# One 512-column matmul per upper weight tile, and loops written out, in a fp32r-split transformer block on one core

## The chip, the core and the metric

The kernel runs on one core of a Trainium2 chip. The metric is device time in microseconds (us), lower is better; the kernel before took 3140.52 us (median of three runs, 3138.92 to 3140.62).

## The reference, cut to what matters

Two transformer-like blocks on 256 tokens with 2048 features, batch 1. The first block is a mixer (a gated delta rule with 8 heads beside a 31-tap convolution), a cross attention over 256 memory tokens and a squared-ReLU MLP:

```python
h = h + hybrid_mixer(rms_norm(h, g), w_in, ...)           # 2048 -> 6160 columns, and w_out
h = h + memory_cross_attention(rms_norm(h, g), mem_n, ...) # four 2048 x 2048 weights
h = h + squared_relu_mlp(rms_norm(h, g), w1, w2)           # 2048 -> 8192 -> 2048
```

The second takes 256 context tokens as well, scales and shifts its norms by a modulation vector (`c @ w_mod`), has latent attention, neighbourhood attention and a Fourier part, an output projection, and a gated MLP with 3-tap convolutions (2048 -> 2 x 5632 -> 2048). All is float32, and nearly all of the work is activations (256 tokens) times weights that are each used once.

## The kernel before, in words

Weights stream from HBM in slots of 128 x 1024 float32 (`raw`, 8 buffers, 906 slots). A float32 product is made of three products in the type fp32r. ScalarE copies a slot to fp32r (`whi`, line 836), VectorE subtracts that from `raw` to get the lower part (`wlo`, line 1233), 4 buffers each. The activations lie in `act` (for the second matrix of each MLP in `hid`) as two parts [P, 2, 16, 256]. For each 128 x 128 weight tile TensorE adds up `whi` x upper, `whi` x lower and `wlo` x upper, three matmuls of 256 columns at line 458, into 256 columns of a bank. In phases marked `flip` the activations are the stationary side and the weight slots are streamed.

A `Phase` is one matrix: `nblocks` blocks of 256 output features, each two halves `hf` of 128, over `chunks` of 128 input features; four chunks are a slot, so a block of a 2048-row matrix takes four slots, 32 tiles and 96 matmuls. Two blocks alternate between banks 0 and 1. A body has `per_body` blocks; a phase of more than one body runs in a hardware loop (`Fori`) on each engine, one of a single body is straight-line code.

`over` writes ScalarE's and VectorE's side of a phase: slot after slot, with the first three slots of a phase split before the phase before is evicted, and a block's eviction `LAG` = 3 slots behind its last slot. Each engine works in this order, so a split written behind an eviction waits for it. Evictions:
- `to`: ScalarE copies the bank to SBUF and frees it (`block_free`).
- `conv4` (phase `qkv`): ScalarE scales the bank by the last tap into `ev` (line 869), VectorE adds three more taps from the bank for each half (line 1252, six instructions) and frees it, ScalarE applies SiLU (line 873).
- `glu`: ScalarE takes the sigmoid of one half (line 880), VectorE multiplies (line 1266).
- `resid`: VectorE adds the bank to `h` (line 1283, or 1287 with a gate); ScalarE squares the result in the last phase ahead of a norm.
- `relu2` (phases `w1`): ReLU, square, upper part on ScalarE, lower part on VectorE.
- `gated` (phases `up`): ScalarE scales and adds a bias (line 901), VectorE adds two taps for each half (line 1308), SiLU (line 906), then product and split on VectorE.

Beside the phases `glu`, `qkv`, `z_0` and `z_1` VectorE also computes the 31-tap convolution (`conv31`, line 1438), one chunk of 128 channels per body, whose first step copies the input (line 1426). Beside `memk` to `w2_3` it sums the modulation (`mod_chunk`, line 1219), with a short group of matmuls (line 476) once in each body.

In order the phases are `glu` (8 blocks), `qkv` (12), `z_0`, `z_1` (2 each), the delta rule, `wout`, `memk`, `memv`, `wq`, cross attention, `wo`, four rounds of `w1` and `w2` (8 blocks each), the small ones of the second block (`ckv`, `nak`, `nav`, `kr` for context and tokens, `cq`, `naq`, `fn`), local attention, `kn` and `v` twice, `qn`, `qr`, latent attention, `wout2`, and three rounds of `up` (16, 16, 12 blocks) and `down` (8 blocks over 16, 16, 12 chunks).

Of the kernel before, what the change touches and what calls it, by code (L numbers as in the profile page):

```python
# [11 lines left out]
ds = bass.ds  # L12


P = 128
# [112 lines left out]
def build(nc, x_t, mem_t, ctx_t, stream, mods, pvec, eye, cmix, catt, na_bias, na_mask, out_t):  # L128
    es = ExitStack()
    with es:  # L130
# [8 lines left out]
        whi = sb("whi", [P, SPL_N, SLOT], F32R)  # L139
        wlo = sb("wlo", [P, SPL_N, SLOT], F32R)  # L140
# [58 lines left out]
        bank = [es.enter_context(nc.psum_tensor(f"bank{i}", [P, 512], F32)) for i in range(8)]  # L199
# [24 lines left out]
        ev_v = sem("ev_v")  # L224
        act_step = sem("act_step")
# [54 lines left out]
        class Chain:  # L280


            def __init__(self, eng, s):
                self.eng, self.s, self.n, self.i, self.per = eng, s, 0, 0, 0

            def __call__(self, ins):
                ins.then_inc(self.s, 1)
                self.n += 1
                self.eng.wait_ge(self.s, self.i * self.per + self.n)
# [6 lines left out]
            def now(self):  # L296
                return self.i * self.per + self.n

            def loop(self, i, per):

                self.n, self.i, self.per, self.mark = self.n - per, i, per, self.n

            def end(self, iters):

                assert self.n == self.mark, (self.n, self.mark)
                self.n, self.i, self.per = self.n + self.per * (iters - 1), 0, 0
# [4 lines left out]
        def over(eng, ph, slot_of, evac_fn, chain, links, extra=None):  # L311
# [21 lines left out]
            if ph.iters > 1:  # L333
                with eng.Fori(1, ph.iters) as i:
                    chain.loop(i, links)
                    body(i, False, 0)
                chain.end(ph.iters)
# [9 lines left out]
        def _(sp):  # L347
# [10 lines left out]
            def bodies(first, last, mod=False):  # L358
                with sp.Fori(first, last) as b:
# [69 lines left out]
        def _(pe):  # L429
            c = Counts(pe)  # L430

            def phase(ph, src, c0=0, after=None):
# [3 lines left out]
                def body(i):  # L436
                    for k in range(ph.K):
                        b = bank[(ph.block0 + k) % 2]

                        pe.wait_ge(block_free, i * ph.K + (ph.block0 + k + 1))  # L440
                        for sl in range(ph.slots_per_block):
# [6 lines left out]
                            for ci in range(ph.per_slot):  # L448
                                kc = sl * ph.per_slot + ci
                                for hf in range(ph.ncol // P if not ph.flip else TT):  # L450
                                    for n, (wx, ax) in enumerate(((whi, 0), (whi, 1), (wlo, 0))):
                                        if ph.flip:
                                            lhs = src[:, ax, c0 + kc, hf * P:(hf + 1) * P]
                                            rhs = wx[:, buf, ci * NCOL:(ci + 1) * NCOL]
                                        else:
                                            lhs = wx[:, buf, ci * ph.ncol + hf * P:ci * ph.ncol + (hf + 1) * P]
                                            rhs = src[:, ax, c0 + kc, :]
                                        mm = pe.matmul(b[:, hf * T:(hf + 1) * T], lhs, rhs,  # L458
                                                       start=(kc == 0 and hf == 0 and n == 0),
                                                       stop=(kc == ph.chunks - 1 and n == 2), skip_group_check=True)  # L460
# [3 lines left out]
                if ph.iters > 1:  # L464
# [324 lines left out]
            for n in range(3):  # L789
                for mt in range(TT):  # L790
                    mm = over_features(bank[5 + n][:, mt * P:(mt + 1) * P], ROOT, 2 * n + mt, mt == 0)
# [34 lines left out]
        def _(sc):  # L826
# [16 lines left out]
            def to(dst, flip=False, func=ACT.Copy):  # L843
                def make(ph):
                    def f(n, b, k):
                        done(ph, n)
                        o = dst[:, 0:TT, ds(n * NCOL, NCOL)] if flip else dst[:, ds(n * 2, 2), :]
                        sc.activation(o, b2(b), func).then_inc(block_free, 1)
# [3 lines left out]
            def one(dst):  # L852
                def make(ph):
                    def f(n, b, k):
                        done(ph, n)
                        sc.activation(dst, bank[b][:, 0:T], ACT.Copy).then_inc(block_free, 1)
# [5 lines left out]

            def conv4(ph):
# [12 lines left out]
            def glu(ph):  # L876
                def f(n, b, k):
                    done(ph, n)
                    sc.wait_ge(block_free, n + (FREE + ph.block0))
                    sc.activation(ev[:, 0, 0:T], b2(b)[:, 1, :], ACT.Sigmoid).then_inc(ev_a, 1)  # L880
                return f

            def relu2(ph):
                def f(n, b, k):
                    done(ph, n)
                    c.at(ev_v, n + EV0)
                    sc.activation(ev[:, 0, :], bank[b][:, :], ACT.Relu).then_inc(block_free, 1)
                    sc.wait_ge(block_free, n + (FREE + ph.block0 + 1))
                    chain(sc.activation(ev[:, 1, :], ev[:, 0, :], ACT.Square))
                    sc.activation(hid[:, 0, ds(n * 2, 2), :], ev[:, 1, :].rearrange("p (a b) -> p a b", a=2),  # L890
                                  ACT.Copy).then_inc(ev_a, 1)
# [995 lines left out]
```

## Time and profile before

| | |
|---|---|
| median of the runs | 3140.52 us |
| profiled execution, span from first to last instruction | 3137.8 us |
| mean granted TensorE clock | 0.972 |
| TensorE matmuls busy | 2967.8 us, 95% |
| VectorE busy | 2097.9 us, 67% |
| ScalarE busy | 1331.5 us, 42% |
| HBM read | 585.88 MB |

TensorE's matmuls are pipelined, so its busy share says that there was always a matmul in flight, not that it ran at its peak; the time from one start to the next has to be worked out from stretches and counts. The chain that ended last tells which work followed on which. Idle time of the other engines costs nothing as long as TensorE finds its slots split and its banks free.

### The profile page before, as it was taken

Reading aid. Unit: us, or ns where it says so; the run is one execution under the profiler, and the core shown is the slowest. Engines: PE = TensorE matmul, PEld = TensorE weight load, DVE = VectorE, ACT = ScalarE, POOL = GpSimd, SP = SyncE. Lnnn points to the kernel's source line nnn. Section 1 sums busy time; section 2 is a strip of 40 time slices with the busy share of each in tenths; the row PEclk is TensorE's granted clock in tenths of the full one; section 3 lists DMA queues with packets and bytes.
Section 4 is the critical chain, followed back from the end, with each engine's and each line's share of the span. In section 5 each row is a group of like instructions: output and inputs, shape, how many; then the busy total and the mean of one; then the engine's idle time right before and its main releaser. Section 6 shows DMA issues by size and latency. Waiting matters only on the chain.

```text
span 3137.8 us, 61329 instructions
## 1 busy us (share of the span) xinstructions
PE 2967.8 (95%) x23858; PEld 2904.4 (93%) x23858; DVE 2097.9 (67%) x2934; ACT 1331.5 (42%) x1646; POOL 5.1 (0%) x13
## 2 busy tenths in 40 slices
PE   7999888999999899999999989979998999999998
PEld 7998788999998899999999979959498999999998
DVE  6988654698877777676776775445456665665565
ACT  4445323343433443444435444435344443444443
POOL 0000000000000000000000000000000000000000
PEclk9999898999999999999999989998899999999999
DMA  5554102577655677777777745514054555556553
GB/s 198 177 171 162 54 1 92 186 265 255 243 201 184 245 277 274 278 275 264 281 268 264 278 132 168 183 60 135 20 181 142 180 195 184 183 187 193 182 185 117
DMA packets 160343, 589.92 MB, mean 188 GB/s; under 512 B 17840, under 2 KB 17840, under 8 KB 159696
## 3 DMA queue, kind: packets, MB, share of 16 engines
q1 hardware_dynamic: 159264, 579.93, 53.8%
q0 software_dynamic: 944, 8.12, 0.7%
q8 instruction: 94, 1.54, 0.2%
q14 instruction: 41, 0.34, 0.0%
HBM read 585.88 MB, written 2.10 MB: 187 GB/s over the span
## 4 chain that ended last, share of the span: by engine, by line
PE 87%; DVE 8%; ACT 3%; issue 2%; DMA 1%; DVEq 0%; SPq 0%; ACTq 0%
PE bank L458 77%; PE bank L725 1%; DVE wlo L1233 1%; PE bank L476 1%; PE bank L482 1%; PE bank L629 1%; DVE modacc L1438 1%; DVE tmp L1388 1%; PE bank L486 1%; DVE ev L1252 1%; PE bank L627 1%; PE bank L621 1%; PE bank L700 1%; DVE ev L1355 1%; ACT whi L836 1%
## 5 line engine op out<-in xcount | busy, mean ns | idle before, releaser
L458 PE MATMUL bank<-act,whi 128*128 128x256 f32 x10144 | 1854.2, 286 | 56.8 <-DVE wlo L1233 16.8
L458 PEld LDWEIGHTS bank<-act,whi 128*128 128x128 f32 x10144 | 1599.7, 194 | 61.8 <-issue 39.5
L1233 DVE TENSOR_TENSOR wlo<-raw,whi 128x1024 fp32r<-128x1024 f32 x906 | 1098.3, 1223 | 538.6 <-ACT whi L836 535.0
L458 PE MATMUL bank<-act,wlo 128*128 128x256 f32 x5072 | 1445.9, 285 | 0.0
L836 ACT ACTIVATE whi<-raw 128x1024 fp32r<-128x1024 f32 x906 | 947.9, 1056 | 918.2 <-PE bank L458 913.0
L458 PEld LDWEIGHTS bank<-act,wlo 128*128 128x128 f32 x5072 | 983.0, 194 | 0.0
L458 PE MATMUL bank<-hid,whi 128*128 128x256 f32 x3456 | 597.1, 278 | 0.0
L458 PEld LDWEIGHTS bank<-hid,whi 128*128 128x128 f32 x3456 | 524.6, 188 | 0.0
L458 PE MATMUL bank<-hid,wlo 128*128 128x256 f32 x1728 | 480.0, 278 | 0.0
L1219 DVE SCALAR_TENSOR_TENSOR modacc<-modraw,small,modacc 128x512 f32<-128x512 f32 x480 | 348.5, 747 | 12.3 <-DMA modraw<-mods 6.9
L458 PEld LDWEIGHTS bank<-hid,wlo 128*128 128x128 f32 x1728 | 324.7, 188 | 0.0
L458 PE MATMUL bank<-whi,act 128*128 128x256 f32 x896 | 161.9, 283 | 0.0
L458 PEld LDWEIGHTS bank<-whi,act 128*128 128x128 f32 x896 | 139.5, 192 | 0.0
L1308 DVE SCALAR_TENSOR_TENSOR ev<-bank,pv,ev 128x255 f32<-128x255 f32 x176 | 76.9, 479 | 92.8 <-ACT ev L901 86.9
L458 PE MATMUL bank<-wlo,act 128*128 128x256 f32 x448 | 126.8, 283 | 0.0
L1438 DVE SCALAR_TENSOR_TENSOR modacc<-modraw,modacc 128x256 f32<-128x256 f32 x232 | 98.6, 480 | 0.3
L458 PEld LDWEIGHTS bank<-wlo,act 128*128 128x128 f32 x448 | 85.8, 192 | 0.0
L901 ACT ACTIVATE ev<-bank,pv 128x256 f32<-128x256 f32 x88 | 44.9, 561 | 91.0 <-PE bank L458 91.0
L914 ACT ACTIVATE ev<-h 128x512 f32<-128x512 f32 (+1 forms) x40 | 25.3, 632 | 117.3 <-DVE h L1283 68.0
L1297 DVE TENSOR_TENSOR hid<-ev,hid 128x512 fp32r<-128x512 f32 x32 | 22.2, 693 | 75.2 <-ACT hid L890 75.2
L906 ACT ACTIVATE ev<-ev 128x256 f32<-128x256 f32 x44 | 18.4, 418 | 89.3 <-DVE ev L1308 89.3
L621 PE MATMUL bank<-tmp 128*128 128x128 f32 x224 | 33.3, 298 | 15.5 <-DVE tmp L1541 8.6
(269 smaller groups left out, 1524.1 us busy)
## 6 DMA issues: line engine op xcount, KB each, us to landing
raw<-stream SPq DMA_DIRECT2D x906, 512.0 KB, 4.5
modraw<-mods SPq DMA_DIRECT2D x192, 512.0 KB, 4.6
h<-x_t SPq DMA_DIRECT2D x4, 512.0 KB, 6.0
memV<-mem_t POOLq DMA_DIRECT2D x1, 2048.0 KB, 9.7
tmp<-ctx_t POOLq DMA_DIRECT2D x1, 2048.0 KB, 12.2
out_t<-tmp SPq DMA_DIRECT2D x4, 512.0 KB, 2.6
cz<-catt POOLq DMA_DIRECT2D x1, 1216.0 KB, 13.2
bias<-na_bias POOLq DMA_DIRECT2D x1, 1024.0 KB, 5.7
```

The costliest lines, as they stand in the source:

```text
L458: mm = pe.matmul(b[:, hf * T:(hf + 1) * T], lhs, rhs, start=(kc == 0 and hf == 0 and n == 0), stop=(kc == ph.chunks - 1 and n == 2), skip_ ...
L476: mm = pe.matmul(bank[2][:, 4 * w + n:4 * w + n + 1], modacc[:, w, n * P:(n + 1) * P], ones[:, 0:1], start=True, stop=True, skip_group_che ...
L482: return pe.matmul(out, src[:, tok], ones[:, 0:1], start=start, stop=stop, skip_group_check=True)
L486: return pe.matmul(out, small[:, col + n:col + n + 1].to_broadcast([P, P]), ident[:, :], start=start, stop=True, skip_group_check=True)
L621: mm = pe.matmul(bk(hg, 0)[:, n, :], MT[hg][:, n, :], X[hg][:, n, :], start=True, stop=True)
L627: pe.matmul(bk(hg, 2)[:, n, :], XT[hg][:, n, :], Y[hg][:, n, :], start=True, stop=True)
L836: sc.activation(whi[:, at % SPL_N, :], raw[:, at % RAW_N, :], ACT.Copy).then_inc(hi_done, 1)
L901: ins = sc.activation(ev[:, 0, hf * T:(hf + 1) * T], b2(b)[:, hf, :], ACT.Identity, scale=par("ff_conv", n * 6 + (6 * first + 3 * hf + 1)) ...
L1219: ins = ve.scalar_tensor_tensor(acc, wt, col, acc, ALU.mult, ALU.add)
L1233: ve.tensor_tensor(wlo[:, at % SPL_N, :], raw[:, at % RAW_N, :], whi[:, at % SPL_N, :].bitcast(F32), ALU.subtract).then_inc(split_done, 1)
L1308: ins = ve.scalar_tensor_tensor(o, b2(b)[:, hf, so], par("ff_conv", n * 6 + (6 * first + 3 * hf + j)), o, ALU.mult, ALU.add)
L1438: ins = ve.scalar_tensor_tensor(acc, x_, w, acc, ALU.mult, ALU.add)
```

## The change

`whi` and `wlo` become halves of one tensor `w2`. For each weight tile the upper part is multiplied by both activation parts at once: one matmul of 512 columns whose moving side is `act[:, :, kc, :]`, into a whole bank; the left half gets upper x upper, the right half upper x lower. The second matmul adds lower x upper (256 columns) to the right half. In `flip` phases the roles are exchanged: 512 columns of `w2[:, :, buf, cols]` are streamed over the upper activations, then 256 of `whi` over the lower. A block needs a bank for each half `hf`, so two blocks take four banks, 0 and 1 and 6 and 7 (`STREAM`), and each eviction has to add the two halves of its banks (`main` and `rest`).

The evictions change so: ScalarE copies `main` and VectorE adds `rest` and frees the banks (`to` with `add`, `one`). In `conv4`, `glu`, `relu2` and `gated` this copy and add come first, in `ev`, and what follows reads SBUF: the scaling by the last tap, the sigmoid, the bias now wait for VectorE's add. `relu2` does ReLU and square in one VectorE instruction. `resid` becomes two passes in a row on `h`. The SiLU of `zT` moves from its evictions to two instructions on ScalarE ahead of the delta rule. All loops (`Fori`) are written out on all engines. Two banks for spreading roots change (5, 2, 4 for 5, 6, 7).

```diff
-                                    for n, (wx, ax) in enumerate(((whi, 0), (whi, 1), (wlo, 0))):
-                                        if ph.flip:
-                                            lhs = src[:, ax, c0 + kc, hf * P:(hf + 1) * P]
-                                            rhs = wx[:, buf, ci * NCOL:(ci + 1) * NCOL]
-                                        else:
-                                            lhs = wx[:, buf, ci * ph.ncol + hf * P:ci * ph.ncol + (hf + 1) * P]
-                                            rhs = src[:, ax, c0 + kc, :]
-                                        mm = pe.matmul(b[:, hf * T:(hf + 1) * T], lhs, rhs,
...
+                                    out = bank[b + hf]
+                                    if ph.flip:
...
+                                        pe.matmul(out[:, :], src[:, 0, c0 + kc, tok], w2[:, :, buf, cols],
+                                                  start=kc == 0, stop=False, skip_group_check=True)
+                                        mm = pe.matmul(out[:, T:2 * T], src[:, 1, c0 + kc, tok], w2[:, 0, buf, cols],
+                                                       start=False, stop=kc == ph.chunks - 1, skip_group_check=True)
+                                    else:
+                                        at = ci * ph.ncol + hf * P
+                                        pe.matmul(out[:, :], w2[:, 0, buf, at:at + P], src[:, :, c0 + kc, :],
+                                                  start=kc == 0, stop=False, skip_group_check=True)
+                                        mm = pe.matmul(out[:, T:2 * T], w2[:, 1, buf, at:at + P], src[:, 0, c0 + kc, :],
+                                                       start=False, stop=kc == ph.chunks - 1, skip_group_check=True)
...
-                if ph.iters > 1:
-                    with pe.Fori(0, ph.iters) as i:
-                        body(i)
-                else:
-                    body(0)
+                for i in range(ph.iters):
+                    body(i)
```

ScalarE's side of `conv4`, and VectorE's side of it and of `to`:

```diff
                     done(ph, n)
-                    sc.wait_ge(block_free, n + (FREE + ph.block0))
+                    sc.activation(halves(ev[:, 1, :]), main(b), ACT.Copy).then_inc(ev_a, 1)
+                    sc.wait_ge(block_free, n + (FREE + ph.block0 + 1))
                     for hf in range(2):
-                        ins = sc.activation(ev[:, 0, hf * T:(hf + 1) * T], b2(b)[:, hf, :], ACT.Copy,
+                        ins = sc.activation(ev[:, 0, hf * T:(hf + 1) * T], ev[:, 1, hf * T:(hf + 1) * T], ACT.Copy,
                                             scale=par("dn_conv", n * 8 + (4 * hf + 3)))
                     ins.then_inc(ev_a, 1)
-                    sc.wait_ge(block_free, n + (FREE + ph.block0 + 1))
-                    chain(sc.activation(qkvT[:, ds(n * 2, 2), :], ev[:, 0, :].rearrange("p (a b) -> p a b", a=2), ACT.Silu))
+                    c.at(taps_done, n + 1)
+                    chain(sc.activation(qkvT[:, ds(n * 2, 2), :], halves(ev[:, 0, :]), ACT.Silu))
...
+            def add(dst, flip=False):
+
+                def make(ph):
+                    def f(n, b, k):
+                        c.at(ev_a, n + 1)
+                        o = dst[:, 0:TT, ds(n * NCOL, NCOL)] if flip else dst[:, ds(n * 2, 2), :]
+                        ve.tensor_tensor(o, rest(b), o, ALU.add).then_inc(block_free, 1)
...
             def conv4(ph):
                 def f(n, b, k):
-                    c.at(ev_a, n + 1)
+                    c.at(ev_a, n * 2 + 1)
+                    ve.tensor_tensor(halves(ev[:, 1, :]), rest(b), halves(ev[:, 1, :]), ALU.add).then_inc(block_free, 1)
+                    c.at(ev_a, n * 2 + 2)
```

ScalarE's side of `glu`, `relu2` and `gated`, and VectorE's `resid` and `relu2`:

```diff
+                    sc.activation(halves(ev[:, 1, :]), main(b), ACT.Copy).then_inc(ev_a, 1)
+                    sc.wait_ge(block_free, n + (FREE + ph.block0 + 1))
+                    sc.activation(ev[:, 0, 0:T], ev[:, 1, T:2 * T], ACT.Sigmoid).then_inc(ev_a, 1)
...
-                    sc.activation(ev[:, 0, :], bank[b][:, :], ACT.Relu).then_inc(block_free, 1)
-                    sc.wait_ge(block_free, n + (FREE + ph.block0 + 1))
-                    chain(sc.activation(ev[:, 1, :], ev[:, 0, :], ACT.Square))
+                    sc.activation(halves(ev[:, 0, :]), main(b), ACT.Copy).then_inc(ev_a, 1)
+                    c.at(taps_done, n + 1)
...
+                        sc.activation(halves(ev[:, 1, :]), main(b), ACT.Copy).then_inc(ev_a, 1)
+                        sc.wait_ge(block_free, n + (FREE + ph.block0 + 1))
...
-                            ve.tensor_tensor(h[:, ds(n * 2, 2), :], b2(b), h[:, ds(n * 2, 2), :], ALU.add).then_inc(block_free, 1)
+                            o = h[:, ds(n * 2, 2), :]
+                            chain(ve.tensor_tensor(o, main(b), o, ALU.add))
+                            ve.tensor_tensor(o, rest(b), o, ALU.add).then_inc(block_free, 1)
...
+                    ve.tensor_tensor(halves(ev[:, 0, :]), rest(b), halves(ev[:, 0, :]), ALU.add).then_inc(block_free, 1)
+                    ve.wait_ge(block_free, n + (FREE + ph.block0 + 1))
+                    ve.scalar_tensor_tensor(ev[:, 1, :], ev[:, 0, :], 0.0, ev[:, 0, :], ALU.max, ALU.mult).then_inc(taps_done, 1)
...
+            sc.wait_ge(block_free, FREE + PH["z_1"].block0 + PH["z_1"].nblocks)
+            for n in range(2):
+                sc.activation(zT[:, 4 * n:4 * n + 4, :], zT[:, 4 * n:4 * n + 4, :], ACT.Silu)
```

## Rows read from the trace of the kernel before

**Rows 1.** The page: busy times, chain by line, an instruction queue, the stream's DMAs.

```profile
PE 2967.8 (95%) x23858; PEld 2904.4 (93%) x23858; DVE 2097.9 (67%) x2934; ACT 1331.5 (42%) x1646; POOL 5.1 (0%) x13
...
PE bank L458 77%; PE bank L725 1%; DVE wlo L1233 1%; PE bank L476 1%; PE bank L482 1%; PE bank L629 1%; DVE modacc L1438 1%; DVE tmp L1388 1%; PE bank L486 1%; DVE ev L1252 1%; PE bank L627 1%; PE bank L621 1%; PE bank L700 1%; DVE ev L1355
...
q8 instruction: 94, 1.54, 0.2%
...
raw<-stream SPq DMA_DIRECT2D x906, 512.0 KB, 4.5
```

**Rows 2.** Chain in order of time: start, length (us), matmul count; one-body phases, `up`, `down`, `w2`.

```profile
1944.90 110.16 PE bank L458 x918
...
2649.94 180.12 PE bank L458 x1501
...
2560.97 85.11 PE bank L458 x751
...
1165.96 29.13 PE bank L458 x257
...
1211.90 31.80 PE bank L458 x270
```

**Rows 3.** Groups of line 458 that read `wlo`: count | busy us, mean ns.

```profile
L458 PE MATMUL bank<-act,wlo 128*128 128x256 f32 x5072 | 1445.9, 285 | 0.0
L458 PE MATMUL bank<-hid,wlo 128*128 128x256 f32 x1728 | 480.0, 278 | 0.0
L458 PE MATMUL bank<-wlo,act 128*128 128x256 f32 x448 | 126.8, 283 | 0.0
```

**Rows 4.** Chain in order of time: float32 matmuls of 256 columns, then of one.

```profile
336.53 3.45 PE bank L567 x16
...
339.99 3.48 PE bank L482 x31
```

**Rows 5.** TensorE's timeline at the start of `glu`; then busy times and clock, `w1_0`.

```profile
40.23 0.41 PE L458 MATMUL bank<-act,wlo 128*128 128x256 f32 x1
...
40.87 0.41 PE L458 MATMUL bank<-act,wlo 128*128 128x256 f32 x1
...
1066.00:1151.00 85.00, 84.90 (x692) 84.93 (x693) 61.90 (x74) 43.28 (x50) 0.53 (x1) 0.97 0.76 280
```

**Rows 6.** Timelines of ScalarE and of VectorE in `qkv`: start, length (us), instructions.

```profile
197.66 0.63 ACT L873 ACTIVATE qkvT<-ev 128x512 f32 x1 [5.35 <-DVE ev L1252]
198.41 3.90 ACT L836 ACTIVATE whi<-raw 128x1024 fp32r<-128x1024 f32 x4
204.07 0.84 ACT L869 ACTIVATE ev<-bank,pv 128x256 f32<-128x256 f32 x2 [1.76 <-PE bank L458]
...
199.50 1.23 DVE L1233 TENSOR_TENSOR wlo<-raw,whi 128x1024 fp32r<-128x1024 f32 x1 [1.98 <-ACT whi L836]
...
207.21 2.68 DVE L1252 SCALAR_TENSOR_TENSOR ev<-bank,modraw,ev 128x255 f32<-128x255 f32 x6
```

**Rows 7.** VectorE's timeline in `glu`: the first step of two bodies' convolution.

```profile
57.00 0.30 DVE L1426 COPY modraw<-cin 128x286 f32 x1
...
104.93 0.30 DVE L1426 COPY modraw<-cin 128x286 f32 x1
```

**Rows 8.** Groups of instructions: an add and a copy of 512 columns from a bank.

```profile
L1283 DVE TENSOR_TENSOR h<-bank,h 128x512 f32<-128x512 f32 (+1 forms) x48 | 33.2, 691 | 18.4 <-PE bank L458 18.2
L848 ACT ACTIVATE kN<-bank 128x512 f32<-128x512 f32 x8 | 4.8, 599 | 13.0 <-PE bank L458 13.0
```

**Rows 9.** Timelines in `up_0`: ScalarE's first pass of an eviction, VectorE's next splits.

```profile
2480.20 1.02 ACT L901 ACTIVATE ev<-bank,pv 128x256 f32<-128x256 f32 x2 [2.12 <-PE bank L458]
...
2485.10 3.49 DVE L1233 TENSOR_TENSOR wlo<-raw,whi 128x1024 fp32r<-128x1024 f32 x3
```

**Rows 10.** Stretches: length; busy PE, PEld, DVE, ACT, POOL; clock, DMA share, GB/s.

```profile
661.00:709.00 48.00, 48.00 (x404) 48.00 (x403) 39.91 (x49) 19.06 (x21) 0.00 (x0) 1.00 0.81 283
...
1153.00:1197.00 44.00, 44.00 (x386) 44.00 (x386) 33.01 (x38) 18.44 (x19) 0.00 (x0) 1.00 0.81 286
```

More of the change, by code:

```diff
@@ L296, in now, with over @@
             def now(self):
[L297 to L306, printed above, removed]
+                return self.n
         block = es.enter_context(nc.Block())
-        def over(eng, ph, slot_of, evac_fn, chain, links, extra=None):
+        def over(ph, slot_of, evac_fn, extra=None):
             ends = [(k + 1) * ph.slots_per_block - 1 + LAG for k in range(ph.K)]
@@ L332, in over @@
             body(0, True, min(PRE, ph.S) if n else 0)
-            if ph.iters > 1:
[L334 to L337, printed above, removed]
+            for i in range(1, ph.iters):
+                body(i, False, 0)
             after = order[n + 1] if n + 1 < len(order) else None
@@ L358, in bodies @@
             def bodies(first, last, mod=False):
-                with sp.Fori(first, last) as b:
+                for b in range(first, last):
                     for j in range(RAW_N):
@@ L951, in _ @@
             phase("glu", glu)
-            phase("qkv", conv4, PH["qkv"].K)
+            phase("qkv", conv4)
+            c.end(taps_done, PH["qkv"].nblocks)
             def row(r):
@@ L1111, in _ @@
             for r in range(FF1_ROUNDS):
-                phase(f"w1_{r}", relu2, PH["w1_0"].K)
+                phase(f"w1_{r}", relu2)
                 c.end(ev_v, PH["w1_0"].nblocks)
+                c.end(taps_done, PH["w1_0"].nblocks)
                 phase(f"w2_{r}", squared if r == FF1_ROUNDS - 1 else nothing)
@@ L1134, in _ @@
             phase("fn", to(fT))
-            phase("kr_x", one(kr[:, 0, :]))
+            phase("kr_x", one(kr[:, 0:1, :]))
             attention("na", 8)
@@ L1259, in f @@
                         if j < DN_TAPS - 1:
-                            ve.wait_ge(dve_step, chain.i * chain.per + chain.n)
+                            ve.wait_ge(dve_step, chain.now())
                 return f
@@ L1323, in gated, with phase @@
                 return make
[L1325 removed]
+            def phase(name, evac, extra=None):
                 ph = PH[name]
[L1327 removed]
+                over(ph, slot, evac(ph), extra)
             def residual(name, gate=None, extra=None):
@@ L1444, in conv31 @@
                 return f
-            CONV_LINKS = 1 + CF_TAPS + 1
             before_qkv = PH["glu"].iters - 1
-            phase("glu", glu, CONV_LINKS, conv31(PH["glu"], -1))
-            c.end(ev_a, 8)
-            phase("qkv", conv4, PH["qkv"].K * 5 + 1 + CONV_LINKS, conv31(PH["qkv"], before_qkv, stage=True))
-            c.end(ev_a, 12)
+            phase("glu", glu, conv31(PH["glu"], -1))
+            c.end(ev_a, 16)
+            phase("qkv", conv4, conv31(PH["qkv"], before_qkv, stage=True))
+            c.end(ev_a, 24)
             for mt in range(TT):
@@ L1454, in _ @@
             ins.then_inc(gate_dve, 1)
-            phase("z_0", nothing, 0, conv31(PH["z_0"], before_qkv + PH["qkv"].iters))
+            phase("z_0", add(zT[:, 0:4, :]), conv31(PH["z_0"], before_qkv + PH["qkv"].iters))
+            c.end(ev_a, PH["z_0"].nblocks)
             c.at(gate_act, 1)
@@ L1461, in _ @@
             ins.then_inc(gate_dve, 1)
-            phase("z_1", nothing, 0, conv31(PH["z_1"], before_qkv + PH["qkv"].iters + 1))
+            phase("z_1", add(zT[:, 4:8, :]), conv31(PH["z_1"], before_qkv + PH["qkv"].iters + 1))
+            c.end(ev_a, PH["z_1"].nblocks)
             assert before_qkv + PH["qkv"].iters + 2 == 8
@@ L1586, in _ @@
             norm(memory, g("norm_mem"))
-            phase("memk", nothing, 0, h_norm(4))
-            phase("memv", nothing)
+            phase("memk", add(memK), h_norm(4))
+            c.end(ev_a, PH["memk"].nblocks)
+            phase("memv", add(memV, flip=True))
+            c.end(ev_a, PH["memv"].nblocks)
             norm(h, g("norm_xa"), ahead=True)
-            phase("wq", nothing)
+            phase("wq", add(tmp))
+            c.end(ev_a, PH["wq"].nblocks)
             def attention(kind, c0=0):
@@ L1635, in _ @@
                 phase(f"w1_{r}", relu2)
-                c.end(ev_a, PH["w1_0"].nblocks)
+                c.end(ev_a, 2 * PH["w1_0"].nblocks)
                 if r == FF1_ROUNDS - 1:
@@ L1737, in _ @@
             for r, n in enumerate(FF2_ROUNDS):
-                phase(f"up_{r}", gated(first), 2 * 5)
-                c.end(ev_a, 2 * n)
+                phase(f"up_{r}", gated(first))
+                c.end(ev_a, 3 * n)
                 first += n
```

164 lines of the change are left out of this document (99 added, 65 removed).

## Prediction

> **What bounds the kernel now.** First the page's busy line and its chain that ended last: TensorE is busy 95% of the span and the streamed matmuls of line 458 alone make 77% of the chain [rows 1]. Busy time says little for a pipelined engine, so next the chain in order of time, divided by its counts: 1501 matmuls in 180.12 us are 120.0 ns each, 918 in 110.16 us again 120.0 ns; where the moving tile is `hid`, 113.3 ns (751 in 85.11 us, 257 in 29.13 us) or 117.8 ns (270 in 31.80 us) [rows 2]. These stretches have no gap. At the full clock of 2.4 GHz, 256 columns take 106.7 ns, so a stretch runs 6.6 to 13.3 ns above its columns for every matmul. Elsewhere another engine sets the pace: in `qkv` the matmuls wait on VectorE and ScalarE (below).
>
> **Part 1, the matmuls.** A 128x128 weight tile costs three matmuls of 256 columns with three weight loads, 3 x 120 = 360 ns on `act`. After the change it is one of 512 and one of 256: the same 768 columns (320 ns), one instruction and one load less. So the columns save nothing, only what stands above them. The trace has no 512-column fp32r matmul. The nearest rows: a float32 matmul pass that occupies the array 213.3 ns, with a weight load each, repeats every 3.45/16 = 215.6 ns; one-column matmuls, which only their loads bound, repeat every 3.48/31 = 112.3 ns [rows 4]. So a load (112) hides wholly under 213 ns, but not quite under 107. I price the 512-column matmul at 215.7 and the 256-column one at today's 120, because the load of the next upper tile can only start beside it: 336 ns a tile, 24 ns less. On `hid` the short one keeps its 113.3 (`down`) or 113.3 to 117.8 ns (`w2`, about 116.1 as a mean: the first 12 of its 32 slots run at the lower rate), so 329 against 340 and 332 against 348.
> The Trainium skill (TensorE: Matmul & The Clock Gate, Back-to-back issue gap) gives columns/2.4 + 2.5 ns, 109.2 and 215.8 ns: an estimate by it is 327.6 ns a tile before and 325.0 after, 2.6 ns saved, which speaks against this change. The trace disagrees for the short matmul (120.0) and agrees for the long one (215.6).
> Counts: the `wlo` rows give one per tile, 5072 + 448 = 5520 tiles on `act` and 1728 on `hid` [rows 3]. Of the first, `glu`, `qkv` and `z` have 24 blocks x 32 = 768, where TensorE will not be the bound; 4752 are left. At the granted half clock (1.2 GHz) a tile takes 0.64 us [rows 5], purely its 768 columns, and that stays. `w1_0` ran at a mean clock of 0.97 over 85 us [rows 5], some 5 us or 8 tiles at half clock; seven such starts make about 60 tiles. Saving: 4692 x 24 = 112.6 us; `w2` 4 x 256 x 16.6 = 17.0; `down` 704 x 11 = 7.7. Sum 137 us.
> Bounds of the tile on `act`: 329 (the short one at the 113.3 seen on `hid`), and 347, if 13.3 ns belong to each load that runs beside a full-rate stream (320 + 2 x 13.3). I take 336, nearest to the two rows.
>
> **Part 2, the mixer's projections.** In `qkv` each block goes round a ring: SiLU on ScalarE (197.66), first split (198.41), VectorE's four lower splits with convolution taps between (199.50 to 207.21), six taps of `conv4` (2.68), SiLU again: 12.4 us [rows 6], against 4 x 8 x 360 ns = 11.5 us of matmuls. TensorE is already late here. The change puts into this ring a VectorE add of 512 columns (0.69, the row of line 1283 [rows 8]) and behind it the two scalings that ran beside VectorE before and now need the sum (0.84 us [rows 6], about 0.95 with both hand-overs). ScalarE's copy of the main halves lies ahead, beside the splits. Round: about 14.0 us, +1.6 x 12 = +19 us. TensorE then needs 10.75 of 14.0 us, so nothing of part 1 shows here.
> In `glu` VectorE's bodies take (104.93 - 57.00)/2 = 24.0 us [rows 7] against 23.0 of matmuls. Twice an add and a wait for the sigmoid behind it (0.42, as a pass of 256 columns in [rows 6], and hand-overs; it was ready before) give 26.2 us a body: +6 over three, less 1 where the first body, without taps, runs faster. `z_0` and `z_1`, one such body each: matmuls 21.5, VectorE as in `glu`, with adds but without the sigmoid, +1. Part 2: +25 us. Bounds: +13, if the bubbles close and only the adds count; +35, if each round also loses a further hand-over.
>
> **Part 3, evictions elsewhere.** Every block gets a ScalarE copy (0.60) and an add (0.69) where it had one [rows 8]; residual blocks get a second pass. Four slots of splits stand ahead of TensorE, so throughput and the time to the next split decide. Throughput: the densest stretch, with the modulation sums, has VectorE busy 39.9 of 48.0 us [rows 10]; with 4 x 0.69 more it is 42.7 of 16 x 8 x 336 ns + 1.68 = 44.7 us. Close, still cover. DMA moves 286 GB/s in `w2` at 0.81 share [rows 10]; 4% faster is 0.85. Time: the gated eviction has the longest chain. Before, from ScalarE's first pass at 2480.20 to VectorE's next split at 2485.10, 4.9 us [rows 9]. Queued behind it on both engines is the split that TensorE wants 3 x 2.69 = 8.06 us after the block's end. The change adds copy 0.65 and add 0.75: 6.3, split finished at 7.5. It just hides, 0.5 us to spare; without that cover it is 44 blocks x the excess. In `relu2` 1.3 us are added to 3.2: hidden. Cost 0.
> Not hidden, since nothing else is ready: the last block of `wout`, `wo`, `w2_3`, `wout2`, `down_2` (five second passes) and of `wq`, `kr_x`, `qr` ahead of attention (three adds), 0.75 each = 6.0; at the end of `z_1` copy and add, 1.4; the SiLU of `zT`, two passes of 1024 columns moved ahead of the delta rule and partly beside VectorE, 1.2. Sum 8.6 us.
>
> **Part 4, loops written out.** TensorE's loops cost nothing now: the 1501 matmuls at 120.0 ns run over their turns. Straight-line code, the phases of one body, runs at the same 120.0 (918 matmuls) [rows 2], so its fetching is hidden there, at half the DMA load of `w2`. Priced 0. New banks (0,1 and 6,7): 0, the waits between phases stand.
>
> **Sum.** -137 + 25 + 9 = -103 us. The profiled execution's span was 3137.8 us, 2.7 below the median of 3140.5; so 3034.5 in a profile and 3037 as median.
>
> **Rivals.**
> A. The excess belongs to loads beside a full-rate stream (347 a tile). For it: `act` and `hid` differ at equal shape, which looks like two reads disturbing each other; the excess is gone at half clock. Against: the fp32 pass with a load each shows 2.3 ns. Time: 4692 x 13.3 = 62, `hid` about 14, so -76 + 34 = 3098. The same page (What happens when you issue a matmul) says the load has a read port of its own and takes none from the stream, which speaks against A; no row here isolates it.
> B. The short matmul also recovers, since the load is never late behind a long one: 329 on `act`: -145 - 28 + 34, 3001 us; with part 2 at its low end 2989.
> C. Slower: the excess grows with columns streamed (a moving read that stalls every few elements). Then 768 columns still cost 360 ns, part 1 is nil, and parts 2 and 3 stay: 3174. It decides as soon as the tile stays above 355 ns. Against it: the short fp32 passes; but they read at half the rate.
> D. Slower: straight-line code at 0.8 DMA share starves an engine. The larger instruction queue moved 94 packets [rows 1]; written out I estimate twice as many. If 28 of them leave TensorE waiting for one landing, 4.5 us in the row of the stream's DMAs [rows 1], that is +125: 3162. Against it: nothing at 0.53 share.
> E. By the skill's gap rule, as a mechanism: the short matmul's 120 would have to be chance; 7248 x 2.6 = 19 saved, 3155. The rows at 120.0 contradict it.
> F. The eviction chains turn out longer and `up` and `w1` stall 1 us a block: 76 blocks, 3037 + 76 = 3113.
>
> **How the numbers follow.** Forecast 0.50 (its own 3015 to 3060), A 0.18, B 0.12, F 0.05, C 0.07, D 0.05, E 0.03. A measurement tells 0.2%, 6.3 us, from no change. Faster: 0.85; slower: C, D, E, 0.14, with 0.01 left for the same. Range 2985 to 3113: it takes in B's low end, A with part 2 at its high end and F, and leaves 0.15 to 0.2 outside.
>
> **What the profile will show.** Right: in `up` two matmuls a tile at 216 and 120 ns, 16 blocks in about 172 us; rounds of 14 us in `qkv` with TensorE waiting on line 1233's successor; 3 us less for a body of `w1`; no gap in `up`. Wrong: a start-to-start of 240 or more for the long matmul (C), 227 (A); VectorE waits inside `up` (F); "issue" ahead of weight loads (D).

## The result, and the profile after

| | before | after |
|---|---|---|
| median of 8 runs each, us | 3140.57 (3138.28 to 3142.02) | 3148.13 (3144.65 to 3153.37) |
| ratio, 95% interval | | 1.0022 (1.0014 to 1.0031) |
| span of the profiled execution, us | 3137.8 | 3146.3 |

The change makes the kernel 0.2% slower; 3037 us was forecast, and 3148 lies above the range. The page of the changed kernel, its lines that answer to [rows 1] and [rows 3] (busy times with counts; chain by line; the queue that moves instructions; groups of instructions):

```profile
PE 2939.3 (93%) x16610; PEld 2538.8 (81%) x16610; DVE 2283.2 (73%) x3244; ACT 1340.6 (43%) x1679; POOL 5.1 (0%) x13
...
PE psum L458 44%; PE psum L460 22%; DVE w L1242 4%; PE psum L452 3%; DVE modacc L1481 2%; PE psum L454 2%; DVE modacc L1228 1%; PE psum L723 1%; DVE ev L1281 1%; ACT w L834 1%; PE psum L627 1%; PE psum L480 1%; DVE tmp L1431 1%; PE psum L474 1%; PE psum L625 1%
...
L458 PE MATMUL psum<-act,w 128*128 128x512 f32 x5072 | 1816.0, 402 | 81.7 <-DVE w L1242 40.8
L460 PE MATMUL psum<-act,w 128*128 128x256 f32 x5072 | 1434.0, 283 | 0.0
...
q8 instruction: 131, 2.15, 0.3%
```

A third of the streamed matmuls and their loads are gone (23858 to 16610 with all others), yet TensorE is busy for only 28 us less. Its share of the chain falls from 87% to 80%, and VectorE's splits rise in it from 1% to 4%. Line 458 idles 81.7 us, of which a split of VectorE ends 40.8, most of it in `qkv`. The start-to-start times say the rest. TensorE's timeline in `down_2` (start, length in us), then the instructions of line 458 in `up_1` and in `cq`:

```profile
3073.05 0.40 PE L458 MATMUL psum<-hid,w 128*128 128x512 f32 x1
3073.29 0.28 PE L460 MATMUL psum<-hid,w 128*128 128x256 f32 x1
3073.41 0.40 PE L458 MATMUL psum<-hid,w 128*128 128x512 f32 x1
3073.64 0.28 PE L460 MATMUL psum<-hid,w 128*128 128x256 f32 x1
3073.76 0.40 PE L458 MATMUL psum<-hid,w 128*128 128x512 f32 x1
```

```profile
L458 PE MATMUL psum<-act,w x454: 395/398/403, 2664.9 to 2825.0; 128*128 128x512 f32 x152
...
L458 PE MATMUL psum<-act,w x64: 391/391/391, 1998.7 to 2020.5; 128*128 128x512 f32 x64
```

The first fence has two tiles in 0.71 us; over the phase a tile takes 353 ns, 235 from the start of the long matmul to the start of the short and 118 to the next long one. The second is a view of line 458 in a stretch (count, shortest, median and longest duration in ns, first and last start): in `up_1` 453 steps of a tile in 160.1 us, 353.4 ns each; in `cq` 63 in 21.8 us, about 347 ns (230 and 117). On `act` a tile was 360, so it lost 7 to 13 ns, not 24; on `hid` it was 340 in `down` and about 348 in `w2`, and became 353. Nothing waits in these stretches: the fault is inside the stream.

The rate can also change within a phase. In `w1_1` a short group of modulation matmuls stands between these two stretches of the same code:

```profile
L458 PE MATMUL psum<-act,w x80: 395/398/403, 1274.9 to 1302.8; 128*128 128x512 f32 x80
...
L458 PE MATMUL psum<-act,w x102: 392/394/395, 1309.7 to 1344.7; 128*128 128x512 f32 x102
```

Ahead of the group 79 steps take 27.9 us, 353 ns each; behind it 101 take 35.0 us, 347 ns.

Phase starts, read from the first matmul of each in the two traces: `qkv` 132.3 to 137.9, `wout` 514.8 to 539.7, `w1_0` 1066.1 to 1086.1, `up_0` 2374.5 to 2379.9, last matmul of `down_2` 3122.2 to 3129.5. So 25 us are lost up to `wout`, some 20 are won back until `up_0`, and `up` and `down` together give 2 us away.

### The profile page after: what moved, and what is told of

It is laid out like the page before. It is cut to its first block, busy times and chain, and to the rows that moved or that the text cites. A ratio compares the mean times of both kernels' runs of the same rounds, so it can differ in the third digit from the quotient of the medians.

```text
span 3146.3 us, 41040 instructions
## 1 busy us (share of the span) xinstructions
PE 2939.3 (93%) x16610; PEld 2538.8 (81%) x16610; DVE 2283.2 (73%) x3244; ACT 1340.6 (43%) x1679; POOL 5.1 (0%) x13
## 4 chain that ended last, share of the span: by engine, by line
PE 80%; DVE 14%; ACT 4%; issue 1%; DMA 0%; SPq 0%; DVEq 0%; ACTq 0%
PE psum L458 44%; PE psum L460 22%; DVE w L1242 4%; PE psum L452 3%; DVE modacc L1481 2%; PE psum L454 2%; DVE modacc L1228 1%; PE psum L723 1%; DVE ev L1281 1%; ACT w L834 1%; PE psum L627 1%; PE psum L480 1%; DVE tmp L1431 1%; PE psum L474 1%; PE psum L625 1%
## 5 line engine op out<-in xcount | busy, mean ns | idle before, releaser
L458 PE MATMUL psum<-act,w 128*128 128x512 f32 x5072 | 1816.0, 402 | 81.7 <-DVE w L1242 40.8
L460 PE MATMUL psum<-act,w 128*128 128x256 f32 x5072 | 1434.0, 283 | 0.0
L1242 DVE TENSOR_TENSOR w<-raw,w 128x1024 fp32r<-128x1024 f32 x906 | 1095.3, 1221 | 340.5 <-ACT w L834 338.3
L834 ACT ACTIVATE w<-raw 128x1024 fp32r<-128x1024 f32 x906 | 933.8, 1054 | 777.4 <-PE psum L460 716.2
L458 PEld LDWEIGHTS psum<-act,w 128*128 128x128 f32 x5072 | 968.4, 191 | 322.2 <-DVE w L1242 41.1
L460 PEld LDWEIGHTS psum<-act,w 128*128 128x128 f32 x5072 | 973.5, 192 | 0.0
L458 PE MATMUL psum<-hid,w 128*128 128x512 f32 x1728 | 611.9, 398 | 0.5 <-DVE hid L1364 0.5
L460 PE MATMUL psum<-hid,w 128*128 128x256 f32 x1728 | 485.6, 281 | 0.0
L458 PEld LDWEIGHTS psum<-hid,w 128*128 128x128 f32 x1728 | 324.9, 188 | 80.6 <-issue 0.8
L460 PEld LDWEIGHTS psum<-hid,w 128*128 128x128 f32 x1728 | 324.4, 188 | 0.0
L452 PE MATMUL psum<-w,act 128*128 128x512 f32 x448 | 158.1, 397 | 0.0
L452 PEld LDWEIGHTS psum<-w,act 128*128 128x128 f32 x448 | 84.1, 188 | 20.1
L454 PEld LDWEIGHTS psum<-w,act 128*128 128x128 f32 x448 | 84.7, 189 | 0.0
```

Source lines behind the costliest of these rows:

```text
L452: pe.matmul(out[:, :], src[:, 0, c0 + kc, tok], w2[:, :, buf, cols], start=kc == 0, stop=False, skip_group_check=True)
L454: mm = pe.matmul(out[:, T:2 * T], src[:, 1, c0 + kc, tok], w2[:, 0, buf, cols], start=False, stop=kc == ph.chunks - 1, skip_group_check=True)
L458: pe.matmul(out[:, :], w2[:, 0, buf, at:at + P], src[:, :, c0 + kc, :], start=kc == 0, stop=False, skip_group_check=True)
L460: mm = pe.matmul(out[:, T:2 * T], w2[:, 1, buf, at:at + P], src[:, 0, c0 + kc, :], start=False, stop=kc == ph.chunks - 1, skip_group_check ...
L834: sc.activation(whi[:, at % SPL_N, :], raw[:, at % RAW_N, :], ACT.Copy).then_inc(hi_done, 1)
L1242: ve.tensor_tensor(wlo[:, at % SPL_N, :], raw[:, at % RAW_N, :], whi[:, at % SPL_N, :].bitcast(F32), ALU.subtract).then_inc(split_done, 1)
```

## The experiments

**Loops alone.** Before with its loops written out and nothing else.

```
-                with eng.Fori(1, ph.iters) as i:
+                for i in range(1, ph.iters):
-                with sp.Fori(first, last) as b:
+                for b in range(first, last):
-                if ph.iters > 1:
-                    with pe.Fori(0, ph.iters) as i:
-                        body(i)
-                else:
-                    body(0)
+                for i in range(ph.iters):
+                    body(i)
```

> The kernel before with nothing changed but the loops written out on all engines. If straight-line code costs nothing (my pricing): 3140 us, within 3 of before. If its fetching is what ate the gain of the matmuls: 3170 us or more.

Measured 3136.91 us, ratio 0.999 (0.9981 to 1.0). Its page:

```profile
q8 instruction: 188, 3.08, 0.4%
```

Twice the packets of [rows 1], and no time lost. Rival D falls.

**The parts of a tile alone.** A kernel of matmuls only, with the rest of the computation left out: once ScalarE has filled the buffers (by 33.5 us), ScalarE, VectorE and the queues are idle. It and the three kernels of its kind below ran once each.

> This kernel leaves the whole computation out: TensorE alone runs stretches of matmuls on fixed data, each stretch a source line of its own, with a weight load before every matmul and ScalarE, VectorE and the DMAs idle. Theory 1 (the stall above 2.4 GHz goes with the columns of the moving fp32r tile, about 10%): 512 columns take 235 ns and 256 take 118 wherever they stand, one piece or two, whether or not the weight tile changes; bfloat16 takes 109 and 216. Theory 2 (the stall goes with each weight load that runs beside a full-rate stream): the excess over the columns is the same 13 to 17 ns for 512 and for 256 columns, so 512 alone takes 227 to 230 ns. Theory 3 (VectorE, ScalarE and DMA traffic in SBUF cause it): with them idle 256 columns take 109 and 512 take 216 ns.

The chain, and then the view of its one line of matmuls in five stretches (count; ns; first and last start; forms):

```profile
33.54 231.42 PE psum L67 x1532
```

```profile
L67 PE MATMUL psum<-act,w x192: 283/283/283, 42.8 to 65.7; 128*128 128x256 f32 x192
...
L67 PE MATMUL psum<-act,w x128: 277/340/403, 65.8 to 88.2; 128*128 128x256 f32 x64, 128*128 128x512 f32 x64
...
L67 PE MATMUL psum<-act,w x59: 389/389/397, 89.7 to 102.9; 128*128 128x512 f32 x59
...
L67 PE MATMUL psum<-hid,w x180: 279/279/280, 133.8 to 154.9; 128*128 128x256 f32 x180
...
L67 PE MATMUL psum<-hid,w x122: 279/338/398, 156.7 to 178.1; 128*128 128x512 f32 x61, 128*128 128x256 f32 x61
```

Three short ones on `act`: 191 steps in 22.9 us, 120 ns each, 360 a tile. Pairs on `act`: one short matmul and 63 pairs from 65.8 to 88.2 us, 353 ns a tile. The long one alone: 58 steps in 13.2 us, 227 ns. On a `hid` 36 bytes off: 117.8 ns, 353 a tile, pairs again 353. These are the kernel's figures with nothing else at work, so no other engine and no DMA makes them, and theory 3 falls. The long one alone is theory 2's; the pair is 7 ns above the 227 + 120 that theory 2 gives. The stretch with a single weight tile also takes 227.

**Undo the merge only.** After, its 512-column matmul made of two of 256; evictions, loops and banks stay as in after.

```
-  pe.matmul(out[:, :], w2[:, 0, buf, at:at + P], src[:, :, c0 + kc, :], ...)
+  for u in range(2):
+      pe.matmul(out[:, u * T:(u + 1) * T], w2[:, 0, buf, at:at + P], src[:, u, c0 + kc, :], ...)
```

> The changed kernel with its 512-column matmul made as two of 256 columns into the two halves of the bank, each with its load; all else as changed. Theory 1 (stall by columns): the tile stays at 353 to 360 ns and the time at 3148 to 3170 us. Theory 2 (stall by loads): a third load adds 13 to 17 ns to 6500 tiles, 3235 to 3260 us.

Measured 3181.97 us, 1.0133 (1.0116 to 1.0149), span 3178.3: 360 ns a tile on `act`, 340 in `down`. That is above theory 1's range and far below theory 2's: the third load costs 7 ns a tile, not 13 to 17. It takes the sum apart. Merging is worth 34 us (3182 to 3148), all the rest of the change costs 41 (3141 to 3182). Phase by phase against after: `up_1` 184.18 to 180.78 us, `wout2` 92.14 to 90.44, `w1_1` 93.81 to 91.11, but `w2_1` 90.76 to 92.09 and `down_1` 86.95 to 90.33.

**Undo the mixer's part.** After, with `glu` and `qkv` as before: three matmuls a tile, their evictions reading the banks.

```
+OLD = ('glu', 'qkv')
+  if ph.name in OLD:
+      for n, (wx, ax) in enumerate(((0, 0), (0, 1), (1, 0))):
+          mm = pe.matmul(bank[b][:, hf * T:(hf + 1) * T], w2[:, wx, buf, at:at + P], src[:, ax, c0 + kc, :], ...)
```

> The changed kernel with glu and qkv as before the change: three matmuls of 256 columns into one bank and the old evictions without the add. If my part 2 was sized right, the time falls by 23 to 27 us to about 3123 us; if the ring of qkv is not what lost the time there, it stays near 3148.

Measured 3123.53 us, 0.9953 (0.9936 to 0.9969). Part 2 costs 24.6 us, where 25 was worked out. The ring, seen in after on ScalarE and VectorE:

```profile
212.19 0.63 ACT L875 ACTIVATE qkvT<-ev 128x512 f32<-128x512 f32 x1 [2.77 <-DVE ev L1281]
218.36 0.60 ACT L868 ACTIVATE ev<-psum 128x512 f32<-128x512 f32 x1 [1.60 <-PE psum L460]
222.38 0.91 ACT L871 ACTIVATE ev<-ev,pv 128x256 f32<-128x256 f32 x2 [3.43 <-DVE ev L1276]
226.07 0.63 ACT L875 ACTIVATE qkvT<-ev 128x512 f32<-128x512 f32 x1 [2.77 <-DVE ev L1281]
...
221.66 0.69 DVE L1276 TENSOR_TENSOR ev<-psum,ev 128x512 f32<-128x512 f32 x1
223.33 2.70 DVE L1281 SCALAR_TENSOR_TENSOR ev<-ev,modraw 128x255 f32<-128x255 f32 x6 [0.98 <-ACT ev L871]
```

SiLU to SiLU is 13.88 us (212.19 to 226.07), against 12.4 in [rows 6]: the add at 221.66, and the scalings that now follow it (222.38), stand in the round.

**And the stages on `hid`.** The same, with `w2` and `down` as before too.

```
-OLD = ('glu', 'qkv')
+OLD = ('glu', 'qkv', 'w2_0', 'w2_1', 'w2_2', 'w2_3', 'down_0', 'down_1', 'down_2')
```

> The kernel e3_old_mix with w2 and down also as before the change (three matmuls, one bank, one pass onto h). In the profile after, a body pair of w2 took 92.1 us against 90.8 before and down 90.3 against 87.0. If the pair is the dearer one on hid wherever it stands: 4 x 1.3 + 2 x 3.4 + 3.3 + about 1 for the last pass = 16 us less than e3, 3107 us. If down and w2 were slower for their evictions: no change from e3's 3123.

Measured 3110.85 us, 0.9898 (0.9881 to 0.9915). The chain in `down_0`:

```profile
2542.57 87.05 PE psum L453 x768
```

768 matmuls at 113.3 ns, 340 a tile: in `down_0` and `down_1` the pair was a loss of 3.4 us each, and without it and without the longer ring the change would have been worth 1%. But the time expected here, 3107, was met in part by luck. The chain in `w2_0` and in `w2_1`, one code on the same addresses:

```profile
1157.18 35.38 PE psum L453 x312
...
1339.27 36.75 PE psum L453 x312
```

`w2_0` starts at 113.4 ns a matmul, `w2_1` at 117.8, 353 a tile; so do `w2_2`, `w2_3` and nearly all of `down_2` (68.46 us, as with pairs). There three short matmuls cost what a pair costs. The rest of the difference between the two traces comes from phases that the edit does not touch: `up_1` and `up_2` ran at 347 ns a tile instead of 353 (6 us less), `up_0` and those before it gave most of that back.

**What decides the 120.** Alone again, each shape and each shift of a buffer on a line of its own; then the same with shifts crossed with the pair and with one or two small float32 matmuls ahead; then with fewer weight columns. The rest of the computation is left out in all three.

> Again only TensorE stretches on fixed data, the whole computation left out, each stretch on lines of its own. The first such kernel gave 120.0 ns for 256 columns alone, 226.7 for 512 alone (both 13.3 above their columns), 109 and 216 for bfloat16, and 353.2 for the pair of 512 and 256, which is 6.5 more than 226.7 + 120.0. If the excess is one stall of 13.3 ns per float32 load beside a full-rate stream and a phase between the load's and the stream's reads adds the rest, the order U0 U1 L0 L1 (two long, then two short) gives 346.7 a tile or anything between 340 and 353, and moving the stream or the weights by a few elements in SBUF changes the 120.0 to other values between 107 and 120, such as the 113.3 seen on hid. If addresses play no part, all stretches of 256 columns stay at 120.0 and the order changes nothing: 353.

> TensorE stretches on fixed data, the whole computation left out: three of 256 columns per tile, and the pair of 512 and 256, with the moving tile 0 to 144 elements behind an address that is a multiple of 1 KB like the weights', each stretch twice behind one or two small float32 matmuls. In the stretches before, 256 columns alone took 120.0 ns at offsets 0 and 64, 113.3 at 4 and 16, 116 to 123 at others. If the relative address sets the stall: three at 4 or 16 take 340 ns a tile against 360 at 0, the pair 333 against 347 to 355. If the address works only for a single repeated form: no difference between offsets in three or pair.

> TensorE stretches on fixed data, the whole computation left out: fp32r streams of 256, 384 and 512 columns with loads of 32, 64, 96 and 128 weight columns, and bfloat16 beside them. If the excess of 13.3 ns is the load's own reading taken from the stream, it shrinks with the columns loaded (about 6.7 at 64, 3 at 32) and is the same at 256, 384 and 512. If it is a fixed cost of an fp32r matmul instruction, it stays 13.3 at 32 weight columns. bfloat16: 2.5 ns throughout.

First kernel: chain (start, us, line, count), then lines by first and last start:

```profile
42.31 15.36 PE psum L73 x128
57.67 14.53 PE psum L77 x64
72.20 13.99 PE psum L81 x128
86.19 13.81 PE psum L85 x64
...
172.80 7.88 PE psum L129 x64
...
188.16 7.25 PE psum L139 x64
...
210.63 7.25 PE psum L154 x64
...
256.02 7.26 PE psum L184 x64
```

```profile
L89 PE MATMUL psum<-act,w x64: 395/398/582, 99.7 to 122.1; 128*128 128x512 f32 x64
...
L218 PE MATMUL psum<-act,w x64: 392/395/579, 344.8 to 366.8; 128*128 128x512 f32 x64
```

Lines 73 and 77 are fp32r, 256 and 512 columns alone: 120.0 and 227.0 ns. Lines 81 and 85 are bfloat16: 109.3 and 215.8. So the price that I gave the long matmul is right for another type. Line 129 shifts the moving tile by 1 element: 123.1 ns. Lines 139 and 154 shift it by 4 and by 16, line 184 shifts the weights by 16: 113.3 ns each. A shift by 64 elements (256 bytes), of either, gives 120 again. Lines 89 and 218 are one piece of code, pairs on the same addresses: 22.4 us for 63 steps and later 22.0, each with a first step of about 0.54 us; past it a tile takes 353 ns and later 347. The order is no lever either: two tiles' long ones, then their short ones, 348 ns a tile; short before long 347, no better than the second stretch in the usual order (the 344.9 and 355.0 that an expectation below names are 347 and 353 in this trace).

Second kernel, the same reading: pairs at a shift of 4 behind one and behind two small matmuls, three short ones at a shift of 48 likewise.

```profile
L135 PE MATMUL psum<-acts,w x40: 387/387/482, 113.4 to 127.0; 128*128 128x512 f32 x40
...
L144 PE MATMUL psum<-acts,w x24: 398/398/482, 127.7 to 136.1; 128*128 128x512 f32 x24
...
L305 PE MATMUL psum<-acts,w x40: 276/276/365, 322.2 to 335.6; 128*128 128x256 f32 x40
...
L315 PE MATMUL psum<-acts,w x24: 281/281/364, 336.3 to 344.5; 128*128 128x256 f32 x24
```

The first tile of each takes some 0.44 us. Past it, pairs take 347 ns and 360 at one shift, three short ones 340 and 353. What ran just before a stream sets its rate for the 24 to 40 tiles of these stretches: pairs differed so at six of eleven shifts, three short ones at three. Over the eleven shifts three short ones took 340 to 360 ns and pairs 347 to 360: of 22 stretches of pairs five at 347, sixteen at 349 to 353, one at 360. The 333 that was expected for a pair at a shift of 4 or 16 did not come.

Third kernel: 256 columns with 32, 64, 96, 128 weight columns, then 384 columns with 128, 512 with 32 and with 128:

```profile
43.77 7.54 PE psum L73 x64
51.31 7.26 PE psum L77 x64
58.57 7.42 PE psum L81 x64
65.99 7.67 PE psum L85 x64
...
107.06 11.11 PE psum L101 x64
...
118.17 14.83 PE psum L105 x64
...
162.44 14.52 PE psum L117 x64
```

117.8, 113.4, 115.9 and 119.8 ns: a quarter of the weights to load is hardly cheaper, and at 512 columns 32 weight columns (line 105, 231.7 ns) are dearer than 128 (226.9), so the excess is not the length of the load. With 128 weight columns 173.6 ns for 384 and 226.9 for 512: about 13.3 ns above the columns at each length. In an even stream the excess goes by the matmul, not by its columns. Every matmul of these streams has a load of its own, so a fixed price of a load and one of a matmul are not told apart.

**Move the buffer in the kernel.** If 120 is a matter of addresses, before has it too, and needs no pairs. `act` moved by 16 elements, what follows it kept in place by a second pad.

```
+        sb("pad_a", [P, 16])
         act = sb("act", [P, 2, DC, T], F32R)
+        sb("pad_b", [P, 240])
```

> The kernel before with act moved by 16 elements (64 bytes) in SBUF and everything behind it kept at its place modulo 1 KB by a second pad; nothing else. If the relative address of stream and weights sets the stall: 5520 tiles on act x 20 ns = 110 us, less where TensorE is not the bound (768 tiles) and at half clock, so 94 us: 3046 us. If addresses play no part in the real kernel: 3140.

Measured 3107.36 us, 0.9881 (0.9858 to 0.9904), 33 us for the 94 expected; its four runs spread over 17 us (3096.79 to 3113.72), and the traced one is the slowest of them. Its chain in `w1_2` and from `up_0` to the end of `down_2`:

```profile
1466.06 45.34 PE bank L460 x384
...
2348.56 747.93 PE bank L460 x6336
```

118.1 ns a matmul where before has 120.3 (46.18 us), not 113.3: on these addresses the stream settles at 353 ns a tile in most phases and at 340 in some. The long chain has the length of before's (747.95 in its trace), though `up_1` fell from 184.18 to 180.79 us: `down_1` rose from 86.95 to 90.33, with `hid` and its weights where they were but for 1 KB. The 26 us that this execution gained stand at the start of `up_0` already (2374.5 to 2348.6): they come from the phases ahead of `up`.

**The same pads in after, and a smaller one in before** (4 and 252 elements), **and the order of the pair** (short before long in after).

> The changed kernel with the same two pads. If the address sets the stall, the pair on act falls from about 353 to about 333 ns: 4690 x 20 = 94 us, 3054 us. If addresses play no part: 3148.

> The kernel before with act moved by 4 elements (16 bytes) instead of 16. In the stretches alone, three per tile took 350 or 340 ns there, by what ran before them, against 353 at 16 and 360 at 0. If the real kernel follows: 3075 to 3105 us, below e5's 3107. If only multiples of 64 bytes help: about 3140.

> The changed kernel with the 256-column matmul of each tile ahead of the 512-column one. In the stretches alone this order took 344.9 ns a tile against 348.4 and 355.0 for the changed kernel's, but the value hangs on what ran before. If the order holds the lower value: -6 ns x 6400 tiles, 3110 us. If only the state at a stretch's start decides: 3140 to 3155, values between 347 and 357 spread as before.

Pads in after: 3161.73 us, 1.0066 (1.0049 to 1.0083), where 3054 was expected if the address decided; pairs take 353 ns nearly everywhere, also in `cq` (349 in `wout2`). Small pad in before: 3116.62, 0.992 (0.9903 to 0.9937), above the 3105 expected; 350 to 355 ns on `act`, but 355 in `down`. Short first: 3149.31, 1.0029 (1.0018 to 1.0041), tiles at 347 and 353 ns: the order brings nothing. No placement and no order brought the pair in the kernel below 347 ns.

## Why the prediction was wrong

**Part 1, the price of the long matmul: the step that failed.** "I price the 512-column matmul at 215.7", from a float32 pass [rows 4]. It measured 226.7 alone and 230 to 236 in pairs. The two rows said 215.6 for 256 columns at the half rate and 120.0 for 256 at the full one; the excess of the type at hand was 13.3, and I gave the long matmul 2.3 because it was long. The figure for the short one (120) was about right (117). Terms, from the phases of the split kernel against after: `act` -46 us where -113 stood, `w2` +5 for -17, `down` +9 for -8; together -32 for -137, the difference of the two spans. The sign on `hid` is the instructive part: its 113.3 was a favourable case of the old stream, which the old stream also lost without a change of its own (the moved `act` lost it in `down`; with the stages on `hid` undone, three short matmuls lost it from `w2_1` on), and the pair did not inherit it.

The Trainium skill (TensorE: Matmul & The Clock Gate, Back-to-back issue gap) gives columns/2.4 + 2.5 ns. The bfloat16 streams agree (109.3, 215.8); the fp32r ones do not (120.0, 226.7). The 215.6 that the prediction took as agreeing was a float32 pass of 256 columns, no 512-column matmul of the type at hand. So rival E fell as a mechanism, though its 3155 us was the nearest to the measured time: it had the saving at 19 us for 32 measured.

**The rivals.** A (347 ns a tile) describes `cq`, `naq`, `fn` and the 13.3 ns per matmul of even streams. Of its reason, the load beside the stream, the part that could be tested does not hold: fewer weights to load leave the excess. Its 3098 missed three things: `hid` dearer by 14 us instead of cheaper by 14 (28), 353 instead of 347 in `up` and elsewhere (16), part 3 (7); with them 3149. C had the right question and the wrong size: it "decides as soon as the tile stays above 355", the kernel has 353, and the split kernel with its 360 ran 3182 where C said 3174. The chance of slower, 0.14, was too low: the bounds of the tile, 329 to 347, left out that the excess in a mixed stream can be larger than in an even one (33.3 ns a tile for 26.7).

**Part 2** held: 24.6 us for 25, a round of 13.88 us for 14.0. By phase starts of the split kernel against before, `glu` cost 4.3 us where 5 stood and `qkv` 17.2 for 19.

**Part 3** held where it was argued closely and was too small in sum. The gated eviction in `up`, answering to [rows 9]:

```profile
2484.59 0.60 ACT L903 ACTIVATE ev<-psum 128x512 f32<-128x512 f32 x1 [1.71 <-PE psum L460]
...
2490.49 3.49 DVE L1242 TENSOR_TENSOR w<-raw,w 128x1024 fp32r<-128x1024 f32 x3
```

5.9 us from copy to next split (6.3 forecast), and no gap on TensorE: in the split kernel, with the new evictions, `up_1` takes the 184.18 us of before. F falls. But what was not hidden cost 41 - 25 = 16 us, not 9. The split kernel's lag on before, read from phase starts, is 24.8 us at `wout`, grows by 9.2 us until `w1_0` and by 6.5 from there to the end. By phase, to the start of the next: `wout` 2.7 us, `wq` 2.1 and `wo` 2.1 where 0.75 stood for each; `memk` 0.9 and `memv` 1.4, for which nothing stood; later `w2_3` 1.5, `wout2` 0.9, `up_0` 1.2, and 2.2 from the start of `down_2` on. Why a hand-over costs more than its add stays open.

**Part 4** held: 0 (ratio 0.999), with twice the instruction packets.

So the forecast failed at one price, that of the long matmul: part 1 gives 105 of the 111 us by which 3148 lies above 3037, part 3 the other 7. Measured: -32 + 25 + 16 = +9 us, the 8.5 of the spans.

## What to carry to other kernels

An operation that no row shows should be bounded by the excess of its own data type and rate before that of a slower pass, and where the gain is only that excess, a kernel of a few hundred bare matmuls in the two arrangements tells it before any rewriting. Merging matmuls at equal columns saved 7 to 13 ns a tile here and was paid for in evictions: restrict it to phases in which TensorE alone sets the pace and where the old stream is slow (3111 against 3148 us here). When a full-rate stream runs some per cent above its columns, try its buffers some bytes further first: a pad of 64 bytes in before gave 1.2% (0.9858 to 0.9904), about what the best form of the change gave (0.9881 to 0.9915). Measure the stream as the kernel has it: at a shift of 16 elements one repeated shape took 113.3 ns, but three matmuls a tile took 353 ns alone and mostly 353 in the kernel, and pairs 349 and 353 in both, so that the same pad made the changed kernel slower (3162 for 3148).

## What the runs showed of the hardware

Full-rate fp32r matmuls of 128 weight columns, back to back, TensorE alone at work: 120.0, 173.5, 226.8 ns for 256, 384, 512 columns; bfloat16 109.2 and 215.8; a float32 pass of 256 columns 215.8. With 128, 192 and 224 columns of fp32r the step is 111.7 each time, so there the load sets it; with 64 weight columns 192 columns take 88.7. The fp32r figure for 256 moved between 113.3 and 123.2 ns with the place of the moving tile or of the weights, the same again after 256 bytes, and, at one place in streams of three, between 113.3 and 117.8 with what ran just before. A pair took 347 ns, the sum of the even streams, in 5 stretches of 22 and mostly 349 to 353; one took 360.

In the kernels with unmoved buffers, nearly every gap-free stretch of 24 tiles takes 340.0, 346.7, 353.3 or 360.0 ns a tile, for three matmuls and for pairs: a ladder with steps of 6.7 ns, on which the pair was found at 346.7 and 353.3 and the three at 340.0, 353.3 and 360.0. With `act` moved by 16 bytes 350 and 355 occur as well, and in the bare kernels some other values. Which step a stream takes goes by addresses and by what ran before it, and a small group of other matmuls is enough to change it (`w1_1` above).

What collides inside the chip, and why a stream keeps the rate at which it starts, stays open; ruled out are the other engines and DMA (idle in the bare kernels), the choice of pieces or of one weight tile, and the amount of weights loaded.
